# Feed-forwards of a two-block float32 model on one Trainium2 core: three parts of 8, 6 and 8 tiles instead of two of 12 and 10

## The chip, the cores and the metric

The kernel runs on one core of a Trainium2 chip, in one launch. The metric is the device time in microseconds (us) of one execution. TensorE (PE) does the matrix products, VectorE (DVE), ScalarE (ACT) and GpSimd (POOL) the elementwise work, and SyncE (SP) issues most of the loads.

## What is computed

The reference, cut to what matters here. Sequence 512, width 1024, feed-forward width 2816; everything is float32.

```python
# first block
h = rms_norm(x, norm_ffn_g) * (1.0 + sc2) + sh2
gt, up = split(h @ w_ffn_up)                  # 1024 -> 2 x 2816
x = x + g2 * ((silu(gt) * up) @ w_ffn_down)   # 2816 -> 1024
# second block, two layers
def conv_glu_ffn(h, w_up, conv_w, conv_b, w_down):
    a, b = split(h @ w_up)
    a = sum(conv_w[j] * shifted(a, j) for j in range(3)) + conv_b
    return (silu(a) * b) @ w_down
for i in range(2):
    x = x + concat(mixer_i(rmsnorm(x, g_mix[i])), memory_attention) @ w_out
    x = x + conv_glu_ffn(rmsnorm(x, g_ffn[i]), ...)
return rmsnorm(x, g_final)
```

There are three feed-forwards: ffn0 in the first block, ffn1 and ffn2 in the second. ffn0 is followed by the projections of the first mixer (the stage a_keys first), ffn1 by two products of the memory (b_mem), ffn2 by the last norm and the output.

## The kernel before

**Precision.** A float32 product is made of three products of a faster type: weight and activation are each split into an upper part and a lower part, and PE sums upper by upper, upper by lower and lower by upper. Every weight tile is so split on the chip: ACT copies it to the upper part (`split_job`, L1613, or L1634 inside a loop), then POOL subtracts (`lower_weights`, L2851).

**Jobs and slots.** The weights of the whole program are a list of jobs (`STAGES`), numbered on; job n uses slot n % 2 of `wslots`, half n % 2 of `w_split` and banks 2p and 2p + 1 for p = n % 2. For job n, SP loads the slot once POOL has done with its last contents; ACT splits it once PE has done job n - 2 (`product_done[p]`), which still reads `w_split[p]`; POOL makes the lower part; PE starts when `lo_ready[p]` says so and the banks have been emptied (`bank_free[p]`).

**A feed-forward** has 22 tiles of 128 hidden units. They are done in two halves (`HALVES`): 12 up jobs (one tile each, gate and up columns side by side: 2 x 8 chunks of K x 3 = 48 matmuls of 128x512), 8 down jobs (128 output columns, 12 chunks x 3 = 36 matmuls), then 10 up jobs and 8 down jobs of 10 chunks (30 matmuls). That is 1,584 matmuls, all issued by `product_of` (L912). The hidden tiles lie in `hid`, 12 tiles of upper and of lower parts.

**After each up job** a chain makes the hidden tile. In ffn1 and ffn2: DVE scales gate and up (L2762, L2763), ACT starts the convolution (L1943), DVE adds two taps (L2767, L2770), ACT applies Silu (L1947), DVE multiplies (L2557), ACT copies the upper part (L1949), DVE subtracts (L2559), gives `hid_ready`, and then gives the job's banks free (L2562). ffn0 has no convolution. The first down job of a half takes the hidden tiles in their order and waits for each (`waits`).

**After each down job** of the first half DVE adds it to x (`residual`, L2516 or L2519). In the last half of ffn0 and ffn1 the next norm is begun there (`late_stage` on ACT, `late_dve` on DVE): DVE adds in the bank (L563, in ffn0 L565), ACT splits the next weights, then makes the upper part of the next stage's input (L509), DVE the lower part (L572), ACT takes the squares (L526, in ffn0 also L522) and copies to x (L527), and only then DVE gives the bank free (`bank_free`). ffn2 only adds and squares.

**The last down stage of ffn1 and ffn2** is issued by `first_downs`: job 0 but for its last chunk, three chunks of job 1, the last chunk of job 0, the rest of job 1. So job 0's last chunk, which waits for the last hidden tile, has work before it. In ffn0 the plain loop is used.

Most of the feed-forward runs in hardware loops of two jobs a turn (`pairs`, a `Fori`), on PE, ACT, DVE and POOL.

## Time and profile before

| | us |
|---|---|
| median of 3 runs | 2096.95 (2092.3 to 2097.04) |
| the profiled execution | 2093.53 |
| its span | 2091.7 |
| PE busy | 2059.9 (98%) |
| DVE, ACT, POOL busy | 989.1, 885.9, 840.6 |
| chain that ended last, on L912 of PE | 72% |

The profiled execution took 1.8 us more than its span; that is what lies around the program's own instructions. The span is the stretch from its first to its last instruction. A matmul of 128x512 is shown as 379 ns long but one starts every 0.216 us; they overlap. So PE's busy share hides small delays, and they are read from the starts of the matmuls. "Idle before" is the time in which the engine did nothing before an instruction, with what ended it behind the arrow.

### The profile page before, as it was taken

To read this page: it belongs to the slowest core of one execution; us is meant where nothing else is said; L and a number is where in the kernel's file an instruction comes from. 1 tells how busy PE (TensorE), PEld (TensorE's weight loads), DVE (VectorE), ACT (ScalarE), POOL (GpSimd) and SP (SyncE) were. 2 spreads that over 40 slices of the span, in tenths; PEclk is the share of its full clock that TensorE was granted. 3 is DMA by queue.
4 is the path that set the end of the run, shared out by engine and by line. 5 is a ranking of instruction groups with operands and counts; after the bars stand their busy time and mean duration, and the time that the engine had idled before them with its cause. 6 is when DMAs were issued, how large, how long until landed. Compare 5 with 4: busy or idle time off the path is not lost.

```text
span 2091.7 us, 28578 instructions
## 1 busy us (share of the span) xinstructions
PE 2059.9 (98%) x10618; PEld 1735.8 (83%) x10618; DVE 989.1 (47%) x1909; ACT 885.9 (42%) x1307; POOL 840.6 (40%) x273
## 2 busy tenths in 40 slices
PE   9999999999999999999999999999999999999998
PEld 6888977888888888876877888888887588888887
DVE  4889788574311111376985344034323934431432
ACT  3355545463443222534366453233423954432332
POOL 3443422444244444433713443444443044444443
PEclk9999999999999999999999999999999999999999
DMA  9654322325232432432202433333422034324322
GB/s 371 243 185 125 102 62 66 101 85 178 81 100 81 114 107 78 113 93 65 79 24 64 113 100 93 107 105 94 143 86 73 2 96 121 100 80 121 100 70 91
DMA packets 304008, 220.17 MB, mean 105 GB/s; under 512 B 13520, under 2 KB 288080, under 8 KB 301616
## 3 DMA queue, kind: packets, MB, share of 16 engines
q1 hardware_dynamic: 293216, 195.67, 31.1%
q10 hardware_dynamic: 10704, 23.33, 3.7%
q8 instruction: 54, 0.88, 0.2%
q14 instruction: 34, 0.28, 0.0%
HBM read 213.48 MB, written 2.10 MB: 103 GB/s over the span
## 4 chain that ended last, share of the span: by engine, by line
PE 85%; DVE 7%; issue 3%; ACT 2%; POOL 2%; DMA 0%; ACTq 0%; DVEq 0%; SPq 0%; POOLq 0%
PE bank L912 72%; PE bank L1159 2%; PE bank L1375 2%; PE bank L1353 2%; DVE arena L2811 1%; PE bank L1307 1%; DVE small L2809 1%; PE bank L1362 1%; PE bank L1458 1%; PE bank L1207 1%; POOL w_split_out L2851 1%; DVE bank L2277 1%; POOL w_split L2851 1%; PE bank L1218 1%; PE bank L1540 1%
## 5 line engine op out<-in xcount | busy, mean ns | idle before, releaser
L912 PE MATMUL bank<-h_hi,w_split 128*128 128x512 f32 x3696 | 1119.4, 382 | 1.8 <-DVE arena L2679 1.1
L2851 POOL TENSOR_TENSOR w_split<-wslots,w_split 128x2048 fp32r<-128x2048 f32 (+3 forms) x174 | 712.7, 4097 | 987.9 <-ACT w_split L1613 549.5
L912 PEld LDWEIGHTS bank<-h_hi,w_split 128*128 128x128 f32 x3696 | 698.7, 189 | 116.8 <-issue 15.7
L912 PE MATMUL bank<-h_lo,w_split 128*128 128x512 f32 x1848 | 701.8, 380 | 0.0
L912 PEld LDWEIGHTS bank<-h_lo,w_split 128*128 128x128 f32 x1848 | 349.7, 189 | 51.2 <-issue 3.4
L912 PE MATMUL bank<-hid_hi,w_split 128*128 128x512 f32 x1056 | 316.2, 380 | 2.2 <-DVEq L2562 2.2
L1634 ACT ACTIVATE w_split<-wslots 128x2048 fp32r<-128x2048 f32 (+2 forms) x80 | 141.4, 1767 | 368.0 <-PE bank L912 368.0
L1613 ACT ACTIVATE w_split<-wslots 128x2048 fp32r<-128x2048 f32 (+3 forms) x91 | 158.8, 1745 | 300.8 <-PE bank L912 278.9
L912 PEld LDWEIGHTS bank<-hid_hi,w_split 128*128 128x128 f32 x1056 | 199.6, 189 | 32.3 <-issue 3.6
L912 PE MATMUL bank<-hid_lo,w_split 128*128 128x512 f32 x528 | 200.1, 379 | 0.0
L2277 DVE SCALAR_TENSOR_TENSOR bank<-arena,cols,bank 128x512 f32<-128x512 f32 x240 | 161.3, 750 | 5.4 <-ACT bank L1727 4.9
L2557 DVE TENSOR_TENSOR bank<-arena,bank 128x512 f32<-128x512 f32 x66 | 45.9, 696 | 210.6 <-ACT arena L1947 210.6
L2851 POOL TENSOR_TENSOR w_split_out<-wslots,w_split_out 128x320 fp32r<-128x320 f32 (+1 forms) x28 | 48.8, 1760 | 183.8 <-ACT w_split_out L1613 183.8
L912 PEld LDWEIGHTS bank<-hid_lo,w_split 128*128 128x128 f32 x528 | 99.8, 189 | 14.0
L2762 DVE TENSOR_TENSOR bank<-bank,rstd 128x512 f32<-128x512 f32 x44 | 30.8, 700 | 138.9 <-PE bank L912 138.5
L2516 DVE TENSOR_TENSOR xT<-xT,bank 128x512 f32 (+1 forms) x24 | 16.5, 688 | 140.0 <-PE bank L912 140.0
L2035 ACT ACTIVATE arena<-arena,small 128x257 f32<-128x257 f32 (+5 forms) x128 | 64.2, 503 | 28.1 <-DVE small L2714 14.9
L2559 DVE TENSOR_TENSOR hid_lo<-bank,hid_hi 128x512 f32 x66 | 45.6, 692 | 57.9 <-ACT hid_hi L1949 57.9
L1949 ACT ACTIVATE hid_hi<-bank 128x512 f32 (+1 forms) x66 | 39.4, 598 | 55.5 <-DVE bank L2557 55.5
L2767 DVE SCALAR_TENSOR_TENSOR arena<-bank,cols,arena 128x511 f32<-128x511 f32 x44 | 33.0, 750 | 58.1 <-ACT arena L1943 58.1
L1353 PE MATMUL bank<-arena 64*128 64x256 f32 (+5 forms) x256 | 54.4, 417 | 4.3 <-DVE small L2704 2.4
L563 DVE TENSOR_TENSOR bank<-bank,xT 128x512 f32<-128x512 f32 x24 | 16.9, 705 | 85.1 <-PE bank L912 85.1
(341 smaller groups left out, 2352.4 us busy)
## 6 DMA issues: line engine op xcount, KB each, us to landing
wslots<-in_f_w_up SPq DMA_DIRECT2D x88, 512.0 KB, 4.7
wslots<-in_w_in SPq DMA_DIRECT2D x24, 1024.0 KB, 5.3
wslots<-in_w_ffn_up SPq DMA_DIRECT2D x44, 512.0 KB, 4.5
arena<-in_w_ada ACTq DMA_DIRECT2D x8, 2048.0 KB, 9.1
wslots<-in_f_w_down SPq DMA_DIRECT2D x16, 768.0 KB, 4.8
wslots<-in_a_w_in SPq DMA_DIRECT2D x10, 1024.0 KB, 5.2
wslots<-in_f_w_down SPq DMA_DIRECT2D x16, 640.0 KB, 4.4
arena<-in_w_ada_first SPq DMA_DIRECT2D x8, 1024.0 KB, 19.3
```

The lines of the kernel that those rows point to most:

```text
L912: return nc.tensor.matmul(bank[:], w, woven(x), start=start, stop=stop)
L1159: last = nc.tensor.matmul(banks[2 * p + b // 2][:, (b % 2) * 2 * P:(b % 2 + 1) * 2 * P], h_split[hp][:, c, b * P:(b + 1) * P], woven(w[wp] ...
L1353: last = nc.tensor.matmul(score_bank(g0 + g, e)[:, 0:n], q, kk, start=True, stop=True)
L1375: last = nc.tensor.matmul(unit_bank(unit)[lo:lo + n, b * P:(b + 1) * P], v, probs_turned[:, (g0 + g) % 3, at:at + P], start=(i == 0), stop ...
L1613: nc.scalar.activation(split_of(JOB_STAGE[n], p)[:, 0, 0:size], slot(p, 1, size)[:, 0, :], ACT.Copy).then_inc(hi_ready[p], 1)
L1634: nc.scalar.activation(split_of(name, p)[:, 0, 0:size], slot(p, 1, size)[:, 0, :], ACT.Copy).then_inc(hi_ready[p], 1)
L1949: nc.scalar.activation(hid[0][:, 0:tiles, :][:, 2 * i + u, :], banks[2 * p][:], ACT.Copy).then_inc(S["hid_hi_ready"], 1)
L2035: last = nc.scalar.activation(part, part, ACT.Exp, bias=stat(n, 2 * with_sink + e), scale=-1.0, accum_out=stat(n, 4 + e))
L2277: ins = nc.vector.scalar_tensor_tensor(out=acc, in0=a_pad[:, c, k:k + T], scalar=dw_w[:, c, k:k + 1], in1=acc, op0=ALU.mult, op1=ALU.add)
L2557: nc.vector.tensor_tensor(halves(banks[2 * p][:]), halves(up_gate[:, p, :]), plain(banks[2 * p + 1][:]), ALU.mult).then_inc(S["hid_made"], 1)
L2559: nc.vector.tensor_tensor(hid[1][:, 0:tiles, :][:, t, :], banks[2 * p][:], hid[0][:, 0:tiles, :][:, t, :].bitcast(F32), ALU.subtract).then ...
L2851: last = nc.gpsimd.tensor_tensor(part[:, 1, cols_of], slot(p, 1, size)[:, 0, cols_of], part[:, 0, cols_of].bitcast(F32), ALU.subtract)
```

## The change

Each feed-forward is done in three parts of 8, 6 and 8 tiles. In the first two parts a down job has two output tiles (256 columns, both banks), so there are four; in the last part there are eight of one output tile, each with 8 chunks. The matmul jobs are then 8 x 48, 4 x 48, 6 x 48, 4 x 36, 8 x 48 and 8 x 24 matmuls, again 1,584, and again 38 jobs, so that slots and banks of all other stages stay as they were.

The last down stage has a new order on PE (`last_downs`), now in ffn0 too. Job 1 uses the second bank of job 0's pair (`down_bank`), so it doesn't wait for the other pair. Job 2's weights are split in two halves.

The loops of the feed-forward on PE, ACT, DVE and POOL are written out. The weights of every odd up job after the first are split in two halves, with the tile's convolution or gate between them on ACT. `up_acc` shares the buffer of `up_gate`. A large part of the diff is for another way to multiply (seven products, entries and token sums); it is governed by `SEVEN`, which is empty, so none of it is issued. Constants and columns get unused space (136 and 24 columns), and the arena is 180 columns smaller.

```diff
-HALVES = ((0, 12), (12, FT - 12))
+PARTS = ((0, 8), (8, 6), (14, FT - 14))
+LAST = len(PARTS) - 1
+DOWN = [P if part == LAST else 2 * P for part in range(len(PARTS))]
+SEVEN = ()
...
+        def down_bank(name, j):
+
+            return banks[2 * one(name, 0)[0] + 1] if j == 1 and name in [f"ffn{k}_down{LAST}" for k in range(3)] else banks[2 * one(name, j)[0]]
...
-                    load(f"ffn{k}_down{half}", n, P, [(0, P, cut(down[:, t0:t0 + n, :], 0, D, P))])
+                    load(f"ffn{k}_down{part}", n, DOWN[part], [(0, DOWN[part], cut(down[:, t0:t0 + n, :], 0, D, DOWN[part]))])
...
-            def first_downs(name, kc, rhs, waits):
+            def last_downs(k, name, kc, rhs, waits):
...
-                for j, (q, first, end) in enumerate(((p, 0, kc - 1), (other, 0, 3), (p, kc - 1, kc), (other, 3, kc))):
...
+                start_split(name, 0)
+                tiles(p, 0, kc - 1)
+                if k == 0:
+                    tiles(p, kc - 1, kc)
+                pe.wait_ge(lo_ready[other], SPLITS_BEFORE[FIRST[name] + 1] + 1)
+                tiles(other, 0, kc - 3)
+                if k:
+                    tiles(p, kc - 1, kc)
+                tiles(other, kc - 3, kc)
+                _, use = one(name, 2)
+                pe.wait_ge(bank_free[p], use + 1)
+                for c in range(kc):
+                    if c == 0:
+                        pe.wait_ge(S["sums_lower"], LOWER[k, "down_half"])
+                    if c == kc // 2:
+                        pe.wait_ge(lo_ready[p], SPLITS_BEFORE[FIRST[name] + 2] + 1)
...
+                for j in range(3, JOBS[name]):
+                    split_job(start_split(name, j), kc, P, rhs, None, 1)
...
             def ffn(k):
...
+                for part, (t0, n) in enumerate(PARTS):
+                    up_part(k, part)
+                    name, rhs, waits = f"ffn{k}_down{part}", lambda c, half: hid[half][:, c, :], ("hid_ready", 2 + FT * k + t0)
+                    if part == LAST:
+                        last_downs(k, name, n, rhs, waits)
+                        continue
+                    for j in range(JOBS[name]):
+                        split_job(start_split(name, j), n, 2 * P, rhs, waits if j == 0 else None)
...
+            def split_down_in_halves(k):
+
+                n = FIRST[f"ffn{k}_down{LAST}"] + 2
+                p, size = n % 2, SIZE[JOB_STAGE[n]]
+                act.wait_ge(weights_in[p], LOADED[n])
+                act.wait_ge(product_done[p], n // 2)
+                for half, done in ((slice(0, size // 2), S["softplus_then_sums_upper"]), (slice(size // 2, size), hi_ready[p])):
+                    nc.scalar.activation(w_split[p][:, 0, half], slot(p, 1, size)[:, 0, half], ACT.Copy).then_inc(done, 1)
...
+            def down_sums(k, part, gate=None):
```

**The order on PE in ffn1, where the first down job waits for the last hidden tiles.** Before, the first down job of ffn1's first half, its last two chunks, and the start of job 1 (w_split_51 and w_split_52 are the two halves of `w_split`):

```order
L912 MATMUL bank<-hid_hi,w_split_51 128x512 [waits hid_ready]
L912 MATMUL bank<-hid_lo,w_split_51 128x512
L912 MATMUL bank<-hid_hi,w_split_51 128x512
L912 MATMUL bank<-hid_hi,w_split_51 128x512 [waits hid_ready]
L912 MATMUL bank<-hid_lo,w_split_51 128x512
L912 MATMUL bank<-hid_hi,w_split_51 128x512
L912 MATMUL bank<-hid_hi,w_split_52 128x512 [waits bank_free1,lo_ready1]
```

With the change, the first down job of ffn1's middle part, its last two chunks, and the start of job 1:

```order
L1034 MATMUL bank<-hid_hi,w_split_51 128x512 [waits hid_ready]
L1034 MATMUL bank<-hid_lo,w_split_51 128x512
L1034 MATMUL bank<-hid_hi,w_split_51 128x512 x2
L1034 MATMUL bank<-hid_lo,w_split_51 128x512
L1034 MATMUL bank<-hid_hi,w_split_51 128x512
L1034 MATMUL bank<-hid_hi,w_split_51 128x512 [waits hid_ready]
L1034 MATMUL bank<-hid_lo,w_split_51 128x512
L1034 MATMUL bank<-hid_hi,w_split_51 128x512 x2
L1034 MATMUL bank<-hid_lo,w_split_51 128x512
L1034 MATMUL bank<-hid_hi,w_split_51 128x512
L1034 MATMUL bank<-hid_hi,w_split_52 128x512 [waits bank_free1,lo_ready1]
```

A chunk now has six matmuls, and there are six chunks instead of twelve: the last wait for a hidden tile has 30 matmuls of the job before it instead of 33.

**The order on PE at jobs 0, 1 and 2 of the last down stage of ffn1.** Before (w_split_51 is job 0, w_split_52 job 1), from the last matmuls of job 0's ninth chunk to those of its tenth:

```order
L912 MATMUL bank<-hid_lo,w_split_51 128x512
L912 MATMUL bank<-hid_hi,w_split_51 128x512
L912 MATMUL bank<-hid_hi,w_split_52 128x512 [waits bank_free1,lo_ready1]
L912 MATMUL bank<-hid_lo,w_split_52 128x512
L912 MATMUL bank<-hid_hi,w_split_52 128x512 x2
L912 MATMUL bank<-hid_lo,w_split_52 128x512
L912 MATMUL bank<-hid_hi,w_split_52 128x512 x2
L912 MATMUL bank<-hid_lo,w_split_52 128x512
L912 MATMUL bank<-hid_hi,w_split_52 128x512
L912 MATMUL bank<-hid_hi,w_split_51 128x512 [waits hid_ready]
L912 MATMUL bank<-hid_lo,w_split_51 128x512
L912 MATMUL bank<-hid_hi,w_split_51 128x512
```

Behind these come 21 matmuls of job 1, then job 2. With the change, from the end of job 0 to the start of job 2:

```order
L1034 MATMUL bank<-hid_lo,w_split_51 128x512
L1034 MATMUL bank<-hid_hi,w_split_51 128x512
L1034 MATMUL bank<-hid_hi,w_split_52 128x512 [waits hid_ready]
L1034 MATMUL bank<-hid_lo,w_split_52 128x512
L1034 MATMUL bank<-hid_hi,w_split_52 128x512
L1034 MATMUL bank<-hid_hi,w_split_52 128x512 [waits hid_ready]
L1034 MATMUL bank<-hid_lo,w_split_52 128x512
L1034 MATMUL bank<-hid_hi,w_split_52 128x512
L1034 MATMUL bank<-hid_hi,w_split_52 128x512 [waits hid_ready]
L1034 MATMUL bank<-hid_lo,w_split_52 128x512
L1034 MATMUL bank<-hid_hi,w_split_52 128x512
L1034 MATMUL bank<-hid_hi,w_split_51 128x512 [waits sums_lower,bank_free0]
```

Job 1's wait for `bank_free1` is gone, and job 2, which waits for job 0's bank (`bank_free0`) and for the first half of its weights (`sums_lower`), starts 9 matmuls after job 0 instead of 21. In ffn0 the change leaves 24 between them.

**The order on ACT at the end of ffn0.** Before, from the split for job 7 to the split for a_keys:

```order
L1613 ACTIVATE w_split_51<-wslots 128x1280 [waits product_done0,weights_in0]
L509 ACTIVATE h_hi<-bank,modg 128x512 [waits resid_ready]
L522 ACTIVATE square<-bank,cols 128x512 [waits late_added,late_ready]
L526 ACTIVATE square<-bank 128x512
L527 ACTIVATE xT<-bank 128x512
L1613 ACTIVATE w_split_52<-wslots 128x2048 [waits product_done1,weights_in1]
```

With the change:

```order
L1779 ACTIVATE w_split_51<-wslots 128x1024 [waits product_done0,weights_in0]
L631 ACTIVATE h_hi<-bank,modg 128x512 [waits resid_ready]
L644 ACTIVATE square<-bank,cols 128x512 [waits late_added,late_ready]
L648 ACTIVATE square<-bank 128x512
L649 ACTIVATE xT<-bank 128x512
L1779 ACTIVATE w_split_52<-wslots 128x2048 [waits product_done1,weights_in1]
```

The split for a_keys keeps its size and its place behind job 6; the job that runs meanwhile, job 7, has 24 matmuls instead of 30.

## Rows read from the trace of the kernel before

**Rows 1.** The page: busy time by engine, granted clock in 40 slices.

```profile
PE 2059.9 (98%) x10618; PEld 1735.8 (83%) x10618; DVE 989.1 (47%) x1909; ACT 885.9 (42%) x1307; POOL 840.6 (40%) x273
PEclk9999999999999999999999999999999999999999
```

**Rows 2.** Windows around ffn0, ffn1, ffn2 (busy by engine, PEclk, DMA); then PE's waits.

```profile
532.00:893.00 361.00, 360.78 (x1671) 315.44 (x1670) 72.38 (x100) 128.06 (x139) 156.85 (x40) 1.00 0.34 95
...
1174.00:1474.00 300.00, 298.90 (x1382) 260.90 (x1383) 103.54 (x145) 112.97 (x113) 129.34 (x31) 1.00 0.36 100
...
1734.00:2034.00 300.00, 298.90 (x1382) 260.89 (x1383) 103.63 (x145) 112.94 (x113) 129.23 (x31) 1.00 0.35 100
...
PE bank L912 <- DVEq L2562: 2.2, 2, 1.1
```

**Rows 3.** PE in two stretches: us, busy (x instructions), PEclk, DMA share, GB/s.

```profile
22.00:200.00 178.00, 177.50 (x921) 1.00 0.63 222
1361.40:1465.00 103.60, 103.60 (x481) 1.00 0.36 100
```

**Rows 4.** PE timeline, ffn1's first down job: start us, us, instruction, [idle before].

```profile
1306.08 0.72 PE L912 MATMUL bank<-hid_hi,w_split 128*128 128x512 f32 x2
1306.63 0.38 PE L912 MATMUL bank<-hid_lo,w_split 128*128 128x512 f32 x1
```

**Rows 5.** PE timeline, ffn1's last down stage, jobs 1 and 2.

```profile
1472.14 0.45 PE L912 MATMUL bank<-hid_hi,w_split 128*128 128x512 f32 x1 [1.10 <-DVEq L2562]
1472.43 0.38 PE L912 MATMUL bank<-hid_lo,w_split 128*128 128x512 f32 x1
...
1479.12 0.82 PE L912 MATMUL bank<-hid_hi,w_split 128*128 128x512 f32 x2
1479.78 0.38 PE L912 MATMUL bank<-hid_lo,w_split 128*128 128x512 f32 x1
```

**Rows 6.** PE timeline, from ffn0's last down job to a_keys.

```profile
884.49 0.38 PE L912 MATMUL bank<-hid_hi,w_split 128*128 128x512 f32 x1
885.10 0.48 PE L912 MATMUL bank<-h_hi,w_split 128*128 128x512 f32 x1 [0.22 <-POOL w_split L2851]
```

**Rows 7.** DVE and ACT timelines, the last hidden tile of ffn1's first half.

```profile
1299.37 0.70 DVE L2762 TENSOR_TENSOR bank<-bank,rstd 128x512 f32<-128x512 f32 x1 [3.48 <-PE bank L912]
...
1305.56 0.69 DVE L2559 TENSOR_TENSOR hid_lo<-bank,hid_hi 128x512 f32 x1 [0.78 <-ACT hid_hi L1949]
```

**Rows 8.** DVE and ACT timelines after job 0 of ffn1's last down stage.

```profile
1475.01 0.70 DVE L563 TENSOR_TENSOR bank<-bank,xT 128x512 f32<-128x512 f32 x1 [3.07 <-PE bank L912]
...
1475.07 1.27 ACT L1613 ACTIVATE w_split<-wslots 128x1280 fp32r<-128x1280 f32 x1 [2.46 <-PE bank L912]
1476.24 0.67 ACT L509 ACTIVATE h_hi<-bank,cols 128x512 fp32r<-128x512 f32 x1
...
1478.22 0.59 ACT L527 ACTIVATE xT<-bank 128x512 f32<-128x512 f32 x1
```

**Rows 9.** Timeline of ffn0's last down stage, after job 4.

```profile
865.49 0.77 DVE L565 SCALAR_TENSOR_TENSOR bank<-bank,mod,xT 128x512 f32<-128x512 f32 x1 [3.72 <-PE bank L912]
...
869.34 0.60 ACT L527 ACTIVATE xT<-bank 128x512 f32<-128x512 f32 x1
```

**Rows 10.** POOL's and ACT's splits by form: busy us, mean ns | idle before.

```profile
L2851 POOL TENSOR_TENSOR w_split<-wslots,w_split 128x2048 fp32r<-128x2048 f32 x121 | 552.1, 4563 | 754.4 <-ACT w_split L1613 416.5 <-ACT w_split L1634 337.9
L2851 POOL TENSOR_TENSOR w_split<-wslots,w_split 128x512 fp32r<-128x512 f32 x4 | 5.0, 1282 | 6.0 <-ACT w_split L1613 6.0
L1634 ACT ACT_TABLE_LOAD x15 | 19.2, 1283 | 0.3
```

**Rows 11.** DMA: instruction queues (packets, MB, share); down loads (KB each, median us to landing).

```profile
q8 instruction: 54, 0.88, 0.2%
q14 instruction: 34, 0.28, 0.0%
...
wslots<-in_f_w_down SPq DMA_DIRECT2D x16, 640.0 KB, 4.4
```

More of the change, by code:

```diff
@@ L55 @@
 SPREADS = 5 + HEADS
-HALVES = ((0, 12), (12, FT - 12))
+PARTS = ((0, 8), (8, 6), (14, FT - 14))
+LAST = len(PARTS) - 1
+DOWN = [P if part == LAST else 2 * P for part in range(len(PARTS))]
+SEVEN = ()
 def ffn_stages(k):
-    return [(f"ffn{k}_{what}{half}", jobs) for half, (_, n) in enumerate(HALVES) for what, jobs in (("up", n), ("down", DT))]
+    return [(f"ffn{k}_{what}{part}", jobs) for part, (_, n) in enumerate(PARTS) for what, jobs in (("up", n), ("down", DT if part == LAST else DT // 2))]
 STAGES = [
@@ new lines, in lower_counts, with sum_counts @@
+def lower_counts():
+    n, at = 0, {}
+    for k in range(3):
+        if k in SEVEN:
+            n += 4 if k else 6
+            for part, (_, tiles) in enumerate(PARTS):
+                for i in range(tiles // 2):
+                    if seven_at(k, part, i):
+                        at[k, part, i] = n
+                        n += 6
+        n += 1
+        at[k, "down_half"] = n
+    return at
+def sum_counts():
+    n, at = 4, {}
+    for k in SEVEN:
+        at[k] = n
+        n += 4
+        for part, (_, tiles) in enumerate(PARTS):
+            for i in range(-1, tiles // 2):
+                if seven_at(k, part, i + 1) and (i >= 0 or part):
+                    at[k, part, i + 1] = n
+                    n += 4
+                if seven_at(k, part, i) and k == 0:
+                    n += 1
+                    at[k, part, i, "late"] = n
+    return at
@@ new lines, in ffn @@
+                    if part < LAST:
+                        for j in range(JOBS[down]):
+                            n = slot_after(FIRST[down] + j)
+                            if seven_at(k, part + 1, 0) and n == FIRST[f"ffn{k}_up{part + 1}"]:
+                                sum_uppers(k, part + 1, 0)
+                                block_uppers(k, part + 1, 0)
+                            else:
+                                split_job(n)
+                if k == 2:
+                    take = squares("last")
+                    for j in range(DT):
+                        if j == 0:
+                            split_down_in_halves(2)
+                        elif j + 2 < DT:
+                            split_job(FIRST[down] + j + 2)
+                        take(j // 2, j % 2, *one(down, j))
@@ L2569, in _ @@
+            if 0 in SEVEN:
+                token_sums_made(0)
+            for part, (t0, tiles) in enumerate(PARTS):
+                up_part(0, part, lambda t, between: hidden(t0 + t, t, one(f"ffn0_up{part}", t)[0], between))
+                if part < LAST:
+                    down_sums(0, part, 5)
             steps.did(nc.vector.tensor_tensor(modg[:, 0, :], cols[:, COL["final_g"]:COL["final_g"] + DT], cols[:, COL["g_mix"]:COL["g_mix"] + DT], ALU.mult))
             steps.settle()
-            late_dve(dve, steps, "a_mix", "ffn0_down1", 5)
+            late_dve(dve, steps, "a_mix", f"ffn0_down{LAST}", 5)
@@ L2752, in ffn, with turn @@
             def ffn(k):
-                for half, (t0, tiles) in enumerate(HALVES):
+                for part, (t0, tiles) in enumerate(PARTS):
                     w3, _ = conv3_of(k, t0, tiles)
-                    for i, u, p, use in pairs(dve, f"ffn{k}_up{half}"):
-                        if u == 0:
-                            steps.loop(i, 2)
-                        t = 2 * i + u
+                    def turn(t, between):
+                        p, use = one(f"ffn{k}_up{part}", t)
                         n = FT * k + t0 + t
```

475 lines of the change are left out of this document (388 added, 87 removed).

## The prediction

> **What bounds the kernel now.** I read the page first: PE is busy for 98% of the span at the full granted clock, in every slice, and no other engine for half of it [rows 1]. So only what keeps PE from starting its next matmul counts. The windows around the feed-forwards come next: PE is busy 360.78 of 361 us in ffn0 and 298.90 of 300 us in each of ffn1 and ffn2, and the one named wait of 1.1 us, twice in all, is most of the rest [rows 2]. The pace is read from a stretch without any wait: 480 matmuls of ffn1's second up stage (the row counts 481) in 103.60 us [rows 3], 0.216 us each. The reader should see that the feed-forwards are a row of matmuls at that pace with a few short breaks, and that the change keeps all 1,584 matmuls of each. It can gain the breaks and lose new ones, nothing else. A break costs more than its "idle before": a matmul is shown 0.38 us long and is due after 0.216, so the start is late by the idle time and 0.16 us more, and the next one comes some 0.1 us late too.
>
> The breaks of before, from the starts in the timeline of PE:
> - ffn1's first down job, at its last chunk. The second matmul of the pair at 1306.08 and the one at 1306.63 are together 0.12 us behind the pace [rows 4]. The hidden tile they wait for was ready at 1305.56 + 0.69 = 1306.25 [rows 7].
> - ffn1's last down stage, job 1: idle 1.10, so 1.26 late, and 0.29 instead of 0.216 to the next: 1.34 us. Job 2, at 1479.12 to 1479.78, takes 0.66 where three starts at the pace would take 0.43: 0.23 us [rows 5]. ffn1 loses 0.12 + 1.34 + 0.23 = 1.69 us. ffn2 has the first two of these, and nothing at job 2: 1.46 us.
> - ffn0, before a_keys: the last matmul of job 7 starts at 884.49, so a_keys is due at 884.71; it starts at 885.10 [rows 6]. With 0.10 at the next, 0.49 us.
> Sum before: 3.64 us.
>
> **The change, part by part.**
>
> *First part (8 tiles, down jobs of 48 matmuls).* The last hidden tile is ready 1306.25 - 1299.37 = 6.9 us after DVE begins with it [rows 7], 7.1 after the first down job starts. Its split is now 2048 columns instead of 1536, which delays the convolution's start by at most 0.5 us. The last chunk comes after 42 matmuls, 9.07 us. No break; the 0.12 us of ffn1 and of ffn2 go.
>
> *Middle part (6 tiles, down jobs of 36).* The last chunk comes after 30 matmuls instead of 33: it is due 0.65 us sooner, the tile is not. The break is 0.12 + 0.65 = 0.77 us in each of ffn1 and ffn2. In ffn0 the chain has neither the scaling nor the convolution, five of its nine steps fewer, and is covered. The up stage behind it needs a split of 2048 columns after job 2: the handover of [rows 6] is 6.48 + 0.39 = 6.87 us from one start to the next, and job 3 lasts 36 matmuls, 7.77 us. Covered.
>
> *Last part, job 1.* Its bank is now free from the start, so the 1.34 us go, in ffn1 and ffn2. Its weights: split and lower part of 1024 columns, about 3.6 us by halving the 4.56 us on POOL [rows 10] and its ACT share, against 21 matmuls, 4.53 us. Covered.
>
> *Last part, job 2 in ffn1.* This is the new wait. Job 0 ends after 39 matmuls of the stage (8.42 us), job 2 is due after 48 (10.36 us), and it must wait for job 0's bank. That bank comes free after the whole late chain: DVE starts on it at 1475.01, ACT's copy to x ends at 1478.22 + 0.59 = 1478.81, 3.80 us later [rows 8]. The split ahead of the chain was 1.17 us to the next instruction; two halves of 512 columns take about as long as two activations of that size, 0.5 to 0.6 us each, so 3.7 to 3.8 us. DVE starts 0.2 us after PE's last matmul has been followed by the next, and giving the bank free takes 0.2. So job 2 may start at 8.42 + 0.2 + 3.7 + 0.2 = 12.5 us: 2.15 us late, 2.25 with the next matmul. Queued behind it on PE is everything; ACT and DVE have job 1's chain to do meanwhile, so nothing else is delayed.
>
> *The same in ffn2.* There DVE only adds (0.7 us) and gives the bank free. The other condition decides: the first half of the weights, ACT 0.6 and POOL 1.28 us for 512 columns [rows 10], with hand-overs 2.15 us after PE's end of job 0, against 9 matmuls, 1.94 less the 0.2. About 0.5 us.
>
> *The same in ffn0.* Between job 0 and job 2 lie 24 matmuls, 5.18 us. The late chain there ends 869.34 + 0.60 - 865.49 = 4.45 us after DVE's start [rows 9], with hand-overs 4.85 us. Covered, by 0.3 us only; this is the thinnest cover of the change, and it holds for each later job too. If it fails it costs what it is over, once in two jobs.
>
> *End of ffn0.* The split for a_keys takes as long as before, but job 7 has 24 matmuls instead of 30, 1.30 us less to hide it. The break grows from 0.49 to 1.79 us. All that follows, the mean of the norm too, is issued behind a_keys on PE, so nothing gives it back. Behind ffn1 two memory products stand in the stream before the next split is needed; behind ffn2 comes no split.
>
> *Loads.* Down loads of 640 KB land in 4.4 us [rows 11]; 512 KB in the last part take no longer and have a period of two jobs, 10.36 us, less 3.6 us for the split. Covered. SP's issues stay in the same places of its queue.
>
> *DVE, ACT, POOL.* One more pass of adds to x, 8 of 0.7 us per feed-forward, beside PE's jobs. In the loops of before, a table of ACT's functions was loaded anew in each turn of the first up stage, 15 times at L1634 for 1.28 us [rows 10]; written out they go. They lie beside up jobs of 10.36 us for which no one waits: nothing.
>
> Sum after: ffn0 1.79; ffn1 0.77 + 2.25 = 3.02; ffn2 0.77 + 0.5 = 1.27: 6.08 us, against 3.64. The change costs **2.4 us**. The profiled execution took 2093.53 us (its span and 1.8 us around it), and so becomes 2096.0; the median of the runs shown is 3.4 us above it and would become 2099.4. I take 2098. The bounds of the sum: if no new break comes, -3.6 us; if the thin cover of ffn0 is missed by 0.5 us in all three pairs and ffn1's chain is 0.5 longer, +5 us.
>
> **The loops.** PE's loop stretch of [rows 3] has four backward branches and not one break. The Trainium skill (Runtime: NRT & Kernel Launch, section Instruction fetch mechanics) says that a taken branch breaks the sequential prefetch, and that kernels prefer full unrolling; by that rule the change would gain at every turn. The trace shows no such cost to regain on PE, and the sum stands on the trace.
>
> **The rivals.** A difference of over 0.3% (6.3 us) is about what a measurement can tell from none.
> - *Faster by the written-out loops.* PE takes 41 backward branches in the three feed-forwards (turns less one of each loop: 15, 13 and 13). If each hid as much as the smallest break that is listed, 0.22 us [rows 6], 9 us would come back: 2090. Against it stands the unbroken stretch. 3%. It is what the rule above would make of it.
> - *Slower by instruction fetch.* Written out, about 3,500 more matmuls are stored, where 7,100 are stored now. The trace has 54 + 34 packets of instructions [rows 11]; in proportion, at most 43 more. The point from which it decides is 0.15 us of PE per packet; at 0.3 us the time is 2111. Against it: the stretch of 22 to 200 us, written out already and with DMA busy 0.63, loses 0.5 us in 921 matmuls [rows 3], which hold some 11 packets, so 0.05 us each. 5%. The Trainium skill (the same section) says that crossing a block is mostly hidden; the trace agrees.
> - *The late chain becomes the bound.* If the chains of ffn0 and ffn1 take 1.2 us longer than read, each of three pairs of jobs loses about 1 us: +6 on the sum, 2104. For it: the 0.3 us of cover. 8%, and half of that passes the 0.3%.
> - *The change doesn't do what it says.* The order shows the three parts and none of the seven products, so this has no chance of its own.
>
> **How the numbers follow.** The forecast has 84%: no difference that can be told. The runs shown span 4.7 us, so even there a median could stray over 6.3 us, rarely. Faster 3%, same 88%, slower 9%. Range 2091 to 2107: the forecast with the spread of the runs below, the late-chain case and the spread above; both loop cases are mostly left out.
>
> **What would show it.** Right: no named PE wait at job 1 of the last down stage; one of about 2 us at job 2 in ffn1 (L1034 of the new kernel) that ends with a bank given free by DVE, 0.3 to 0.4 in ffn2 ended by POOL, none in ffn0; 0.5 to 0.6 idle at the middle part's first down job, twice; 1.5 idle before a_keys. ACT's busy time falls by the 19 us of the table loads at least, without effect. Wrong: many small idle times named "issue" on PE (fetch), a wait at every second job of ffn0's last down stage (late chain), or a pace other than 0.216 us.

## The result, and the profile after

| | before | after |
|---|---|---|
| median of 20 runs, us | 2095.57 | 2098.89 (2095.35 to 2103.06) |
| profiled execution, us | 2093.53 | 2095.35 |
| its span, us | 2091.7 | 2093.5 |

The ratio is 1.0017, with a 95% interval from 1.001 to 1.0024: slower by 3.3 us in the medians, where 2.4 us were forecast, and inside the 0.3% that count as the same. (One of the 20 runs of before took 3067.73 us; the ratio is formed without it.) The forecast of the time was 2098 us, in a range of 2091 to 2107. The page of the changed kernel (its first part, the DMA queues, and the issues):

```profile
PE 2059.6 (98%) x10618; PEld 1737.4 (83%) x10618; DVE 1004.4 (48%) x1933; ACT 852.4 (41%) x1307; POOL 847.2 (40%) x300
...
q8 instruction: 81, 1.33, 0.3%
q14 instruction: 39, 0.32, 0.0%
...
wslots<-in_f_w_down SPq DMA_DIRECT2D x8, 1024.0 KB, 5.1
wslots<-in_f_w_down SPq DMA_DIRECT2D x16, 512.0 KB, 3.9
```

PE has the same work in the same share [rows 1]. ACT lost 33 us of busy time (885.9 to 852.4) without effect, as said. The instruction packets rose from 54 and 34 [rows 11] to 81 and 39. So the question is again where PE stands still. Its waits from ffn1's middle part to the memory products, and those of ffn0 and ffn2 in two more answers:

```profile
PE bank L1034 <- DVEq L700: 1.9, 1, 1.9
PE bank L1476 <- DVEq L700: 0.8, 1, 0.8
PE bank L1034 <- DVE hid_lo L2829: 0.2, 1, 0.2
```

```profile
PE bank L1034 <- POOL w_split L3237: 1.5, 1, 1.5
```

```profile
PE bank L1034 <- POOL w_split L3278: 0.3, 1, 0.3
PE bank L1034 <- DVE hid_lo L2829: 0.2, 1, 0.2
```

L700 is where DVE gives a bank free, L1476 is the memory product, L3237 and L3278 are POOL's lower parts. The timeline of PE around five of these six (the second middle part reads as the first):

```profile
885.54 0.48 PE L1034 MATMUL bank<-h_hi,w_split 128*128 128x512 f32 x1 [1.50 <-POOL w_split L3237]
885.86 0.38 PE L1034 MATMUL bank<-h_lo,w_split 128*128 128x512 f32 x1
...
1366.37 0.38 PE L1034 MATMUL bank<-hid_hi,w_split 128*128 128x512 f32 x1
1366.96 0.48 PE L1034 MATMUL bank<-hid_hi,w_split 128*128 128x512 f32 x1 [0.21 <-DVE hid_lo L2829]
1367.28 0.38 PE L1034 MATMUL bank<-hid_lo,w_split 128*128 128x512 f32 x1
...
1484.69 0.38 PE L1034 MATMUL bank<-hid_hi,w_split 128*128 128x512 f32 x1
1487.00 0.48 PE L1034 MATMUL bank<-hid_hi,w_split 128*128 128x512 f32 x1 [1.92 <-DVEq L700]
1487.32 0.38 PE L1034 MATMUL bank<-hid_lo,w_split 128*128 128x512 f32 x1
...
1517.97 0.38 PE L1034 MATMUL bank<-hid_hi,w_split 128*128 128x512 f32 x1
1519.18 0.89 PE L1476 MATMUL bank<-arena 128*128 128x256 f32 x3 [0.83 <-DVEq L700]
...
2048.37 0.38 PE L1034 MATMUL bank<-hid_hi,w_split 128*128 128x512 f32 x1
2049.04 0.46 PE L1034 MATMUL bank<-hid_hi,w_split 128*128 128x512 f32 x1 [0.29 <-POOL w_split L3278]
2049.33 0.38 PE L1034 MATMUL bank<-hid_lo,w_split 128*128 128x512 f32 x1
```

Read as in the prediction, start less start less 0.216 us, with the next matmul:

| break | forecast | after | from |
|---|---|---|---|
| before a_keys | 1.79 | 1.77 | idle 1.50 + 0.16, next 0.10 |
| ffn1, middle part | 0.77 | 0.48 | 0.59 - 0.22, next 0.10 |
| ffn1, job 2 | 2.25 | 2.20 | 2.31 - 0.22, next 0.10 |
| before the memory product | none | 0.99 | 1.21 - 0.22 |
| ffn2, middle part | 0.77 | 0.48 | as in ffn1 |
| ffn2, job 2 | 0.5 | 0.53 | 0.67 - 0.22, next 0.07 |
| sum | 6.08 | 6.45 | |

Less the 3.64 us of before that is 2.8 us (2.6 with the 0.17 us at ffn2's job 2, two starts in 0.60 us, that the reading of before passed over; the break of 0.5 us at the first up job of ffn1 and of ffn2 isn't listed either, but both kernels have it). The two spans differ by 1.8 only: the first long stretch began 0.8 us sooner in the profile of after, and each profile holds one of the half-clock periods of which the last section tells, behind another stage.

**The wait that was missed.** ACT before and after it (the first row of the first fence is of the kernel before, the second fence is of after), and SP's loads:

```profile
1512.19 1.91 ACT L1613 ACTIVATE w_split<-wslots 128x2048 fp32r<-128x2048 f32 x1 [2.44 <-PE bank L912]
```

```profile
1514.56 1.91 ACT L1779 ACTIVATE w_split<-wslots 128x2048 fp32r<-128x2048 f32 x1 [2.94 <-DMA wslots<-in_b_w_in]
1516.38 0.67 ACT L631 ACTIVATE h_hi<-bank,cols 128x512 fp32r<-128x512 f32 x1
...
1518.36 0.59 ACT L649 ACTIVATE xT<-bank 128x512 f32<-128x512 f32 x1
```

```profile
1502.01 0.41 SPq L948 DMA_DIRECT2D arena<-in_w_mem_kv  x1
1506.60 5.55 SPq L857 DMA_DIRECT2D wslots<-in_b_w_in  x2
```

```profile
1497.80 0.48 SPq L826 DMA_DIRECT2D arena<-in_w_mem_kv  x1
1503.69 7.13 SPq L735 DMA_DIRECT2D wslots<-in_b_w_in  x2
```

The 2 MB of memory weights are issued just ahead of b_q's 1 MB: in after at 1502.01 and 1506.60, in before (last fence) at 1497.80 and 1503.69. b_q's weights landed 7.9 us after their issue (in before 7.2), against medians of 5.1 to 5.4 for this size elsewhere. The time to landing of that one load, first after, then before:

```profile
DMA to landing us min/median/max: 7.9/7.9/7.9
```

```profile
DMA to landing us min/median/max: 7.2/7.2/7.2
```

Before, they were issued 8.5 us ahead of the split that wants them; now only 5 us, because jobs are 24 matmuls long, not 30. ACT works in order: it stood 2.94 us for them, so job 6's chain came late, its copy to x ended at 1518.95, and the bank on which the memory product waits came free then.

### The profile page after: what moved, and what is told of

The parts are those of the page before. It is cut to its first block, busy times and chain, and to the rows that moved or that the text cites. A ratio compares the mean times of both kernels' runs of the same rounds, so it can differ in the third digit from the quotient of the medians.

```text
span 2093.5 us, 27399 instructions
## 1 busy us (share of the span) xinstructions
PE 2059.6 (98%) x10618; PEld 1737.4 (83%) x10618; DVE 1004.4 (48%) x1933; ACT 852.4 (41%) x1307; POOL 847.2 (40%) x300
## 4 chain that ended last, share of the span: by engine, by line
PE 86%; DVE 7%; issue 2%; ACT 2%; POOL 1%; DMA 0%; ACTq 0%; DVEq 0%; SPq 0%; POOLq 0%
PE bank L1034 72%; PE bank L1328 2%; PE bank L1541 2%; PE bank L1519 2%; DVE arena L3193 1%; PE bank L1476 1%; DVE small L3191 1%; PE bank L1528 1%; PE bank L1624 1%; PE bank L1376 1%; POOL w_split L3237 1%; DVE bank L2544 1%; PE bank L1387 1%; PE bank L1706 1%; POOL w_split_out L3237 0%
## 5 line engine op out<-in xcount | busy, mean ns | idle before, releaser
L3237 POOL TENSOR_TENSOR w_split<-wslots,w_split 128x2048 fp32r<-128x2048 f32 (+3 forms) x147 | 598.4, 4072 | 851.2 <-ACT w_split L1779 839.6
L1779 ACT ACTIVATE w_split<-wslots 128x2048 fp32r<-128x2048 f32 (+2 forms) x142 | 247.6, 1744 | 602.3 <-PE bank L1034 577.6
L3237 POOL TENSOR_TENSOR w_split_out<-wslots,w_split_out 128x320 fp32r<-128x320 f32 (+1 forms) x28 | 48.8, 1761 | 185.3 <-ACT w_split_out L1779 185.3
L3287 POOL TENSOR_TENSOR w_split<-wslots,w_split 128x1024 fp32r<-128x1024 f32 x24 | 57.3, 2386 | 118.5 <-ACT w_split L2194 118.5
L2194 ACT ACTIVATE w_split<-wslots 128x1024 fp32r<-128x1024 f32 x24 | 25.5, 1062 | 116.1 <-PE bank L1034 116.1
L2934 DVE TENSOR_TENSOR xT<-xT,bank 128x512 f32<-128x512 f32 x32 | 20.6, 684 | 103.3 <-PE bank L1034 103.3
L2829 DVE TENSOR_TENSOR hid_lo<-bank,hid_hi 128x512 fp32r<-128x512 f32 x66 | 45.6, 692 | 44.4 <-ACT hid_hi L2165 44.4
L2165 ACT ACTIVATE hid_hi<-bank 128x512 fp32r<-128x512 f32 x66 | 39.4, 597 | 47.6 <-DVE bank L2825 47.6
L3289 POOL TENSOR_TENSOR w_split<-wslots,w_split 128x1024 fp32r<-128x1024 f32 x24 | 57.2, 2382 | 0.0
```

Of the source, the lines that this page charges most:

```text
L1779: nc.scalar.activation(split_of(JOB_STAGE[n], p)[:, 0, 0:size], slot(p, 1, size)[:, 0, :], ACT.Copy).then_inc(hi_ready[p], 1)
L2829: nc.vector.tensor_tensor(hid[1][:, t, :], banks[2 * p][:], hid[0][:, t, :].bitcast(F32), ALU.subtract).then_inc(S["hid_ready"], 1)
L3237: last = nc.gpsimd.tensor_tensor(part[:, 1, cols_of], slot(p, 1, size)[:, 0, cols_of], part[:, 0, cols_of].bitcast(F32), ALU.subtract)
L3287: nc.gpsimd.tensor_tensor(w_split[p][:, 1, 0:half], raw[:, 0:half], w_split[p][:, 0, 0:half].bitcast(F32), ALU.subtract)
L3289: nc.gpsimd.tensor_tensor(w_split[p][:, 1, half:], raw[:, half:], w_split[p][:, 0, half:].bitcast(F32), ALU.subtract).then_inc(lo_ready[p], 1)
```

## Experiments

Two more numbers are read here for each kernel. Each run comes with its span and its mean granted clock; span x clock is an estimate of the span that it would have at the full clock, as long as PE makes the time. The clock is given to 0.001 (2.1 us), so one run says little, but its mean over the runs of the kernel before was 2088.2, 2088.0 and 2088.1 us in three sets (27, 33 and 21 runs). For the changed kernel it is 2091.2 (20 runs) and 2090.8 (11 runs). The other experiments have 11 runs each, job 1 in the other pair only 5; the standard error of a mean is 0.2 to 0.5 us, with 5 runs 0.7.

"Breaks" is the sum of what PE's starts are late in the one profile of each kernel, from the second job of each feed-forward to the product behind it, read as in the prediction and without what half-clock periods stretch.

| kernel | ratio to before, interval | mean clock | span x clock, us | breaks, us |
|---|---|---|---|---|
| before | 1 | 0.9974 to 0.9979 | 2088.1 | 3.8 |
| after, first time | 1.0017 (1.0010 to 1.0024) | 0.9972 | 2091.2 | 6.5 |
| after, again | 1.0021 (1.0012 to 1.0030) | 0.9972 | 2090.8 | 6.0 |
| before with its loops written out | 1.0002 (0.9993 to 1.0011) | 0.9977 | 2087.9 | 3.7 |
| job 1 in the other pair | 1.0043 (1.0029 to 1.0057) | 0.9972 | 2094.5 | 10.6 |
| job 2 in a free pair | 1.0005 (0.9996 to 1.0014) | 0.9980 | 2089.7 | 4.8 |
| parts of 6, 6, 10 | 1.0021 (1.0012 to 1.0030) | 0.9969 | 2090.3 | 5.8 |
| memory weights early | 1.0021 (1.0012 to 1.0030) | 0.9969 | 2089.7 | 5.5 |
| a_keys in halves | 1.0017 (1.0008 to 1.0026) | 0.9972 | 2089.8 | 4.9 |
| job 2, memory and a_keys together | 1.0005 (0.9996 to 1.0014) | 0.9976 | 2088.1 | 3.5 |
| the same, memory in quarters | 0.9987 (0.9978 to 0.9996) | 0.9976 | 2086.2 | 2.5 |
| before, job 1 in the same pair | 0.9985 (0.9976 to 0.9994) | 0.9979 | 2086.1 | 1.1 |

The ratios of the last two rows are to the set of before with the lowest clock (0.9974, median 2095.5 us, where the other two sets have 2094.1 and 2093.9). By span x clock they are 0.9991 and 0.9990 of the kernel before.

**The kernel before, its feed-forward loops on PE and ACT written out.**

```diff
+            if name.startswith("ffn") and any(eng is x for x in written_out):
+                for i in range(first, JOBS[name] // 2 if end is None else end):
+                    for u in range(2):
+                        yield i, u, (n0 + u) % 2, (n0 + u) // 2 + i
+                return
```

> The kernel before, with the loops of the three feed-forwards written out on PE and ACT and nothing else changed. Theory of the breaks: writing out costs PE nothing and gives nothing, so PE's named waits in the feed-forwards are those of before (1.10 us twice, 0.22 us once), the ratio to the kernel before is 1.000 (within 0.0007), and only ACT's busy time falls, by the table loads (about 30 of 1.28 us, 38 us). Rival, instruction fetch: the instruction queue carries some 25 packets more and PE shows idle times of its own; if fetch makes up the difference of 3.3 us between the two kernels, the ratio is 1.0016. Rival, backward branches: up to 9 us faster, 0.996.

1.0002. q8 carried the same 81 packets as in after, and PE's waits are those of before:

```profile
PE bank L920 <- DVEq L2571: 1.1, 1, 1.1
```

The same stands at job 1 of ffn2, and the 0.2 us ahead of a_keys. So the branches cost PE nothing that shows, and 27 more packets on q8 cost nothing either, where 3.3 us were to be explained and 9 us were the rival's. Both loop rivals fall.

**Job 1 in the other pair, as before the change.**

```diff
-            return banks[2 * one(name, 0)[0] + 1] if j == 1 and name in [f"ffn{k}_down{LAST}" for k in range(3)] else banks[2 * one(name, j)[0]]
+            return banks[2 * one(name, j)[0]]
...
-                            last = product_of(banks[2 * p + (q != p)], w[q][wp][:, c, :], rhs(c, hp), c == 0 and wp + hp == 0, c == kc - 1 and wp == 1)
+                            last = product_of(banks[2 * q], w[q][wp][:, c, :], rhs(c, hp), c == 0 and wp + hp == 0, c == kc - 1 and wp == 1)
...
-                pe.wait_ge(lo_ready[other], SPLITS_BEFORE[FIRST[name] + 1] + 1)
+                start_split(name, 1)
```

> The changed kernel, but job 1 of each last down stage in its own pair of banks again, with the wait for it. Theory of the breaks: in ffn1 and ffn2 job 1 is due 4.53 us after the stage begins and its bank is free at about 7.0, so a wait of 2.3 to 2.6 us comes at job 1 in each (idle before 2.2 to 2.4), none in ffn0; job 2 of ffn1 stays 9 matmuls behind job 0 and waits about 1.9 idle as before. 4.6 to 5.2 us slower than the changed kernel, about 2103.8, ratio to the kernel before 1.0040. Rival: the second bank gives nothing, since the last hidden tile ends the wait anyway: then as the changed kernel, 1.0017.

In ffn1 and the memory:

```profile
PE bank L1034 <- DVEq L700: 1.9, 1, 1.9
PE bank L1034 <- issue: 1.8, 1, 1.8
PE bank L1476 <- DVEq L700: 0.8, 1, 0.8
```

Job 1 now waits 1.8 us (so it does in ffn2) where 2.2 to 2.4 were expected, job 2's wait stays as long as it was, and span x clock is 3.4 us above the changed kernel (4.6 to 5.2 expected; the waits of the trace come to 4.1). The second bank is what keeps job 1 from costing; job 2's wait doesn't come from it.

**Job 2 in a free pair.** Jobs 2 and 3 of ffn1's last part use the pair that job 1 left free, so job 2 needn't wait for job 0's bank.

```diff
+            if name == f"ffn1_down{LAST}" and j in (2, 3):
+                return banks[2 * one(name, 1)[0] + j - 2]
...
-                pe.wait_ge(bank_free[p], use + 1)
+                if k == 1:
+                    pe.wait_ge(bank_free[other], one(name, 1)[1] + 1)
+                else:
+                    pe.wait_ge(bank_free[p], use + 1)
```

> The changed kernel, but jobs 2 and 3 of ffn1's last down stage use the other pair of banks, which is long free, so job 2 does not wait for job 0's bank. Theory: the wait of 1.92 us idle at job 2 of ffn1 is for the bank; what is left is the wait for the first half of the weights, 0.3 us idle as in ffn2. 1.6 to 1.7 us less than the changed kernel, about 2097.2, ratio to the kernel before 1.0008. The wait of 0.8 us idle before the memory's first product stays: it is for ACT, which waits for a load. Rival: the late chain itself is the bound of the stage, and the time comes back at jobs 4 to 7 or before the memory's product (that wait grows to 2.5): then as the changed kernel, 1.0017.

```profile
PE bank L1487 <- DVEq L702: 0.9, 1, 0.9
PE bank L1036 <- POOL w_split L3289: 0.3, 1, 0.3
```

The wait fell from 1.9 to 0.3, now for the weights, and span x clock fell by 1.4 us of the 1.6. The wait ahead of the memory product stayed at 0.9: it isn't a consequence of job 2's.

**Parts of 6, 6 and 10 tiles.**

```diff
-PARTS = ((0, 8), (8, 6), (14, FT - 14))
+PARTS = ((0, 6), (6, 6), (12, FT - 12))
```

> The changed kernel with parts of 6, 6 and 10 tiles instead of 8, 6 and 8 (10 hidden tiles of space). Theory: there are two down stages whose last chunk comes after 30 matmuls, so the wait of 0.21 us idle stands twice in ffn1 and in ffn2 (+0.48 us each, +0.96 in all); job 7 has 30 matmuls again, so the wait before a_keys falls from 1.50 to 0.22 us idle (-1.28), and the load for the mixer behind ffn1 has 6.48 us a job again, so the wait of 0.83 us idle before the memory's first product goes (-1.0); job 2 of ffn1 is still 9 matmuls behind job 0 and keeps its 1.9 us. Sum -1.3 us, about 2097.6, ratio to the kernel before 1.0010. Rival, the number of parts or written-out code costs, not the length of the last jobs: as the changed kernel or slower, 1.0017 to 1.0022.

```profile
PE bank L1034 <- DVEq L700: 2.1, 1, 2.1
```

```profile
PE bank L1034 <- POOL w_split L3278: 0.7, 1, 0.7
```

The memory product's wait went, and that ahead of a_keys fell to 0.2: with 10 chunks in a job the cover is that of the kernel before. The wait of 0.2 at the first down job came twice in ffn1 and in ffn2, as expected. But job 2's waits grew: in ffn1 (first fence) from 1.9 to 2.1, in ffn2 (second fence) from 0.3 to 0.7. So the breaks fell by 0.7 us and not by the 1.3 expected, and span x clock fell by 0.8. The ratio, 1.0021, is not the 1.0010 that was expected; it is what the rival (the number of parts costs) had forecast, 1.0017 to 1.0022. What speaks against the rival is the trace: the waits that were to go went, and the clock of 0.9969 hides it in the ratio.

**Memory weights early.** The 2 MB are issued between the loads of jobs 4 and 5.

```diff
+                    if k == 1 and part == LAST:
+                        for j in range(DT):
+                            load_one(f"ffn1_down{part}", j, n, P, [(0, P, cut(down[:, t0:t0 + n, :], 0, D, P)[:, :, j, :])])
+                            if j == 4:
+                                load_mem(1)
+                        continue
...
-            load_mem(1)
```

> The 2 MB of memory weights are issued between the loads of jobs 4 and 5 of ffn1's last part, so that they are through before b_q's weights set out. Theory (the memory product waited because b_q's weights shared the DMA engines with the 2 MB, ScalarE stood for them and could not make the copy that frees the bank): b_q's load lands within 5.5 us of its issue, ScalarE's idle 2.94 us goes, the idle 0.83 us ahead of the memory product goes, and the time falls by 1.0 us against the changed kernel, to a ratio of 1.0012. Rival 1 (the bank is late because the jobs are 5.18 us apart and VectorE and ScalarE are loaded): b_q's weights come early, the idle 0.8 us stays. Rival 2 (the 2 MB only delay something else): job 5's own weights come late, and TensorE is idle up to 4 us there, for a ratio of 1.0025 or more.

PE's waits in the stretch, and ACT's for a load:

```profile
PE bank L1039 <- DVEq L700: 1.9, 1, 1.9
```

```profile
ACT w_split L1784 <- DMA wslots<-in_f_w_down: 2.1, 1, 2.1
```

The wait ahead of the memory product is gone, b_q's load landed after 5.3 us, and span x clock fell by 1.4 us. So it was the load. But ACT now stood 2.1 us for a job's weights: the 2 MB crowd whatever comes behind them. The ratio, 1.0021, didn't move to the 1.0012 expected, since the mean clock was lower.

**a_keys in halves.** ACT and POOL split its weights in two halves of four chunks, and PE starts on the first.

```diff
+                    elif n == FIRST["a_keys"]:
+                        act.wait_ge(weights_in[n % 2], LOADED[n])
+                        act.wait_ge(product_done[n % 2], n // 2)
+                        for part, done in ((slice(0, SLOT // 2), S["softplus_then_sums_upper"]), (slice(SLOT // 2, SLOT), hi_ready[n % 2])):
+                            nc.scalar.activation(w_split[n % 2][:, 0, part], slot(n % 2, 1, SLOT)[:, 0, part], ACT.Copy).then_inc(done, 1)
```

> a_keys' weights, 8 chunks, are split in two halves of 4 on ScalarE and GpSimd, and TensorE starts on the first. Theory (the 1.50 us ahead of a_keys are GpSimd's one long lower half, begun when ScalarE had its upper half and 4.5 us long): the first half of it is 2.3 us long, is there some 2 us sooner, and the idle 1.50 us goes wholly, 1.77 us with what a wait costs beside it: ratio to the kernel before 1.0009. Rival (a_keys then waits for its late tiles or for its second half, which is begun no sooner): half the idle stays, 0.5 to 1.0 us at the start or at chunk 4, and the ratio stays at 1.0013 to 1.0017.

```profile
PE bank L1039 <- issue: 0.2, 1, 0.2
```

The 1.5 us became 0.2, span x clock fell by 1.3 us. By the waits the rival falls; the ratio alone, 1.0017 where 1.0009 was expected, is still inside the rival's 1.0013 to 1.0017.

**The changed kernel again.** No edit.

> The changed kernel itself, on the chip on which the next three run, so that they have it beside them. If the 1.0017 is the change's own, this gives 1.001 to 1.0024 again, with the same idle spells of TensorE: 1.50 us before a_keys, 0.2 ahead of the two middle parts, 1.9 ahead of ffn1's job 2 of the last part, 0.3 at ffn2's, 0.8 ahead of the memory product. If what differs from chip to chip is the length of the program's periods at the half clock, the spells are the same and the ratio moves by up to 1.7 us (0.0008) for each period that it has more or fewer than the kernel before.

The same waits but one: ahead of the memory product 0.42 us instead of 0.83 (0.61 in the run of a_keys in halves), so that one varies with how the loads fall. The ratio is 1.0021, and span x clock agrees within 0.4 us.

**Job 2 in a free pair, memory weights early and a_keys in halves together.**

> Job 2 of ffn1's last part in a free pair of banks, the memory weights early and a_keys in halves, together. If the waits found are the whole cost of the change, this takes off 1.6 + 1.0 + 1.8 = 4.4 us of it: about 2094.5 us where the changed kernel has 2098.9, a ratio to the kernel before of 0.9998 (0.999 to 1.0005), and TensorE's idle spells of over 0.1 us in the ffns are 0.2, 0.2, 0.3 and 0.3. That would show that parts of 8, 6 and 8 with jobs of two tiles cost nothing in themselves and gain nothing either. If other waits follow on those that go, the ratio is 1.0005 to 1.0012.

```profile
PE bank L1046 <- DVEq L707: 0.8, 1, 0.8
```

```profile
ACT w_split L1806 <- DMA wslots<-in_f_w_down: 3.8, 1, 3.8
```

Span x clock 2088.1, that of the kernel before, and 3.0 us below the changed kernel instead of 4.4: a new wait of 0.8 us for a bank had come, behind an ACT that stood 3.8 us for job weights issued next after the 2 MB. So the ratio, 1.0005, lies where the expectation and its rival (other waits follow) meet, and the trace says that the rival is in part right.

**The same, the 2 MB in quarters** of 512 KB, one behind each load of jobs 3 to 6.

```diff
-                            if j == 4:
-                                load_mem(1)
+                            if 3 <= j < 7:
+                                load_mem(1, 2 * (j - 3))
```

> As the run with all three edits, but the 2 MB of memory weights go in four transfers of 512 KB, one behind each load of jobs 3 to 6 of ffn1's last part. There the 2 MB in one piece held up the next job's own 512 KB (landed after 7.9 us instead of 4), ScalarE stood 3.79 us for them, and TensorE stood 0.83 us for a bank at 1501.74. Theory (a transfer of 2 MB takes its neighbour's share of the DMA engines wherever it is put, and 1 MB per job of 5.18 us is little enough): neither b_q's nor any job's load lands over 5.5 us after its issue, ScalarE has no wait for a load there, both the 0.83 us at a job and the 0.83 us ahead of the memory product are gone, and the time is 1.0 us below the run with all three edits: a ratio to the kernel before of 1.0000 (0.9991 to 1.0009). Rival (the bank is late for the chain's own length, a load only shows in it): a wait of 0.4 us or more for a bank stays in jobs 5 to 7 or before the memory product, ratio 1.0005.

```profile
PE bank L1048 <- POOL w_split L3312: 0.3, 1, 0.3
```

Both waits for a bank are gone, b_q's load landed after 5.2 us, and span x clock is 4.9 us below the changed kernel, against 4.4 worked out. The ratio of 0.9987 is better than the 0.9991 to 1.0009 expected, in part because of the low clock of its set of before; it is clear of 1, but the difference still counts as the same. The Trainium skill (DMA: Bandwidth & Descriptors, section Queues, rings and completion order) says that each DMA engine takes the descriptors of a ring in order. What was seen agrees: the load behind the 2 MB is the one that suffers, whichever it is (b_q's 7.9 us, or a job's 7.9 where 3.9 is the median), and it stops with pieces of 512 KB.

**The kernel before, job 1 in the same pair.** Parts of 12 and 10, and of the whole change only the second bank for job 1 in ffn1 and ffn2.

```diff
+            return banks[2 * one(name, 0)[0] + 1] if j == 1 and name in ("ffn1_down1", "ffn2_down1") else banks[2 * one(name, j)[0]]
...
-                    if j < 2:
+                    if j == 0:
                         start_split(name, j)
+                    if j == 1:
+                        pe.wait_ge(lo_ready[other], SPLITS_BEFORE[FIRST[name] + 1] + 1)
```

> The kernel before with one idea of the change alone: job 1 of the last down stage of ffn1 and ffn2 goes to the second bank of job 0's pair. Parts of 12 and 10, jobs of 30 matmuls. Theory (the wait of 1.10 us at job 1 is for the other pair's bank and nothing else, and job 2 is no problem here, since with 30 matmuls a job 5.8 us lie between the end of job 0 and job 2 where the change had 1.9): both waits of 1.10 us go, 1.34 us each, nothing comes in their place, and the time falls by 2.7 us below the kernel before: a ratio of 0.9987 (0.998 to 0.9996). Rival 1 (job 2's bank or weights become late as in the changed kernel): an idle time of 0.5 us or more at job 2 in ffn1, and a ratio of 0.999 to 1. Rival 2 (the half-clock periods decide about differences as small as this, and come with the place of the idle spells): the waits are gone in the trace and the ratio is nevertheless 0.9995 or more, with a mean granted clock below that of the kernel before.

The trace names no wait of PE at all in these stretches of ffn1 and ffn2. The ratio is 0.9985; span x clock fell by 2.0 us of the 2.7. So this one part of the change was worth having, and the rest of it, three parts of 8, 6 and 8 above all, took it back. With the waits mended, three parts and two can't be told apart (2086.2 and 2086.1).

## Why the prediction was right, point by point

- **What bounds it.** That PE's breaks make the time is shown: over kernels whose breaks run from 1.1 to 10.6 us, span x clock less the breaks is between 2083.7 and 2085.0 us in all twelve rows of the table. Single steps agree less well (1.4 us where 1.0 was taken away, 4.9 for 4.0, 2.0 for 2.7), with a standard error of some 0.3 to 0.7 us on each.
- **The clock** was misread: "the full granted clock, in every slice" rests on digits that only say 90% or more. The trace of before has a period at half the clock (window, us, PE busy, clock):

```profile
906.00:909.40 3.40, 3.40 (x10) 0.53 0.00 0
```

- **Job 1**, 1.34 us gained in ffn1 and in ffn2: right. No wait there; undoing it cost 3.4 us, doing it alone in the kernel before brought 2.0 of the 2.7.
- **Job 2 in ffn1**, 2.25: measured 2.20. That it is the bank and not the weights is shown by the free pair. **Job 2 in ffn2**, 0.5: 0.53.
- **End of ffn0**, 1.79: 1.77, ended by POOL as said. The halves show that it is the one long lower part.
- **The thin cover in ffn0** held: the only wait between 560 and 890 us is that before a_keys.
- **Middle part**, 0.77 twice, to be seen as 0.5 to 0.6 idle: a mis-sized term, 0.48 measured, with 0.21 idle. The hidden tile was ready 6.6 us after DVE began with it (1360.31 to 1366.21 + 0.69) where the row of before gave 6.9 [rows 7]. DVE's two taps start 0.78 us apart instead of 0.91:

```profile
1360.31 0.70 DVE L3143 TENSOR_TENSOR bank<-bank,rstd 128x512 f32<-128x512 f32 x1 [3.76 <-PE bank L1034]
...
1362.56 0.75 DVE L3148 SCALAR_TENSOR_TENSOR arena<-bank,cols,arena 128x511 f32<-128x511 f32 x1 [0.94 <-ACT arena L2150]
1363.34 0.75 DVE L3151 SCALAR_TENSOR_TENSOR arena<-bank,cols,arena 128x510 f32<-128x510 f32 x1
...
1366.21 0.69 DVE L2829 TENSOR_TENSOR hid_lo<-bank,hid_hi 128x512 fp32r<-128x512 f32 x1 [0.66 <-ACT hid_hi L2165]
```

  The taps are 0.13 us of the 0.29; the rest is in the other hand-overs of the chain. In the kernel with the loops of PE and ACT written out, but not DVE's, the chain still took 6.9 us. What is left is DVE's own loop, or another part of the change such as the buffer that `up_acc` now shares; no run parts the two.
- **Loads**, "Covered", and **"Behind ffn1 two memory products stand in the stream before the next split is needed"**: the step that failed. Only the down loads' own size and period were weighed. The 2 MB that share the DMA engines with b_q's load, with 5 us in place of 8.5 to hide it, were left out, and the memory product needs a bank whose release goes through ACT. It cost 0.6 to 1.0 us in the profiles; moving the 2 MB takes it off.
- **The sum**, 2.4 us: 2.8 by the breaks, 3.0 by span x clock over 31 runs, 3.3 by the medians. The two errors on the breaks, 0.58 too much for the middle parts and 0.99 too little for the memory, nearly cancelled. What the ratio of 1.0021 (4.4 us) holds beyond 3.0 is mostly the clock, to which the prediction gave no term. That 2098.89 came so near to 2098 is luck too: the forecast stood on the median of 3 runs, 2096.95, 1.4 us above that of 20, and 2098 was picked between 2096.0 and 2099.4 without a working.

## What to carry to other kernels

When a job is made shorter, everything that was hidden behind one job gets less cover at once: the split of the next stage's weights, the chain that frees a bank, and the transfer queued behind a large one. List all three for the last job of a stage, where the next stage begins, and not only for a job in its middle. A large load that isn't urgent goes out in pieces between the urgent ones. And a change of several parts is worth taking apart: one of its parts in the old kernel was better here than the whole.

## What the runs showed of the hardware

**Periods at half the clock behind a short standstill.** The profiles hold stretches of some 3.4 us in which PE runs at the lower of its two levels, 1.2 GHz, and matmuls start 0.43 us apart instead of 0.216. Each costs up to half of its length, 1.7 us. Granted clock in three windows of the kernel with job 1 in the other pair (the third column is PE's busy time, the fourth the clock), then PE's first rows in the middle one:

```profile
1480.00:1488.00 8.00, 6.07 (x27) 1.00 0.20 59
1489.00:1492.40 3.40, 3.34 (x8) 0.54 0.53 154
1493.00:1500.00 7.00, 7.00 (x34) 1.00 0.26 75
```

```profile
1489.06 0.62 PE L1034 MATMUL bank<-hid_hi,w_split 128*128 128x512 f32 x1 [1.92 <-DVEq L700]
1489.47 0.64 PE L1034 MATMUL bank<-hid_lo,w_split 128*128 128x512 f32 x1
1489.90 1.06 PE L1034 MATMUL bank<-hid_hi,w_split 128*128 128x512 f32 x2
```

The twelve profiles hold 18 such periods before 2080 us (three of them twice as long), from none in the run of the three edits together to four in that of parts of 6, 6 and 10. All but one begin right behind one of four standstills of PE: 1.58 us long at 905 us, 2.25 us at 1061 us, 1.9 us at 1608 us, all three in every kernel, and the wait at job 2, here at 1489 us and in the parts of 6, 6 and 10 at 1481 us. The 1.50 us ahead of a_keys had none behind it. The same standstill is followed by a period in one profile and not in another. So the wait at job 2 may cost twice. The six sets of runs with a wait of 1.9 us or more at job 2 have mean clocks of 0.9969 to 0.9972, all others 0.9974 to 0.9980; the difference of some 0.0006 is 1.2 us, and closes most of what lies between the breaks and the ratios. The nearest to a test is the kernel with job 2 in a free pair, which took this one standstill away and left the others: 0.9980, against 0.9972 in both sets of the changed kernel, with a standard error of 0.0002 to 0.0003 on each. Memory weights early and a_keys in halves left it in, and their clocks stayed at 0.9969 and 0.9972. So it is likely that this wait lowers the clock; with 11 runs in a set it isn't beyond doubt, and why one execution has the period and another not is open.

The Trainium skill (TensorE: Matmul & The Clock Gate, section A second HAM failure mode: psum-queue depth-cycling) says that short idle spells between groups of matmuls can let the clock go back and forth between its levels. These runs agree in kind, with single spells of 1.6 to 2.3 us and one period, of 3.4 or twice 3.4 us, behind each at most.

**Handovers inside a loop.** On DVE the same two taps start 0.90 us apart in all 44 pairs of the kernel before, where they stand in a hardware loop, and 0.79 us in all 44 of the changed one, where they are written out. No run wrote out DVE's loop and nothing else, so that the loop is the cause isn't shown. On PE no such difference was found: 0.216 us from start to start in both.
